# Two blocks of a transformer on one core: the sums of squares of the norms as two rounded terms, and the input norm's statistic inside the tile behind the head

## The reference, cut to what matters

```
def rms_norm(x, g):
    return x * rsqrt(mean(x * x, axis=-1) + NORM_EPS) * g

for layer in range(2):                       # first block
    h = rms_norm(x, mix_pre_g[layer])
    m = hybrid_swa_rwkv(h, ...) if layer == 0 else nsa_layer(h, ...)
    x = x + rms_norm(m, mix_post_g[layer])
    h = rms_norm(x, ffn_pre_g[layer])
    x = x + rms_norm(conv_ffn(h, ...), ffn_post_g[layer])
# second block
h = h + 0.5 * rms_norm(swiglu(rms_norm(h, g1), ...), g1_post)
u = rms_norm(h, mix_norm_pre)
... attention branch and recurrent branch of u @ w_in, merged ...
h = h + rms_norm(merged @ w_out, mix_norm_post)
h = h + 0.5 * rms_norm(swiglu(rms_norm(h, g2), ...), g2_post)
```

## Time and profile before

| | |
|---|---|
| median of three executions | 2860.36 us |
| the profiled execution's own time | 2854.86 us |
| its span | 2853.1 us |
| TensorE (PE) busy | 97% of the span |
| VectorE busy | 51% |
| ScalarE busy | 37% |
| chain that ended last | PE 92%, DVE 4%, ACT 3%, issue 1%, DMA 0% |

### The profile page before, as it was taken

How to read it: one execution, slowest core, us unless ns; L and a number is a source line. 1 busy time by engine, 2 the same in 40 slices (tenths; PEclk the granted TensorE clock), 3 DMA queues, 4 the chain that set the end, 5 groups by cost and what they waited for, 6 DMA issues and landing times.

```text
span 2853.1 us, 38460 instructions
## 1 busy us (share of the span) xinstructions
PE 2780.3 (97%) x16326; PEld 2251.5 (79%) x16326; DVE 1450.4 (51%) x2394; ACT 1061.3 (37%) x1618; POOL 14.6 (1%) x30
## 2 busy tenths in 40 slices
PE   8988999999999999999999999999999999999997
PEld 6787788888887788888887888877788788888886
DVE  5844576543525756655345443284634444654433
ACT  5534453332325654433233222244333422432221
POOL 0000000000000000000000000001000000000000
PEclk9999999999999999999999999999999999999999
DMA  4200122222421002222223222236222122222221
GB/s 149 89 8 3 45 89 96 96 89 96 155 100 36 1 1 96 96 96 89 96 74 111 89 96 96 89 115 123 78 78 85 67 96 96 89 90 95 96 91 65
DMA packets 68861, 238.84 MB, mean 84 GB/s; under 512 B 7976, under 2 KB 10536, under 8 KB 68180
## 3 DMA queue, kind: packets, MB, share of 16 engines
q1 hardware_dynamic: 62064, 220.41, 22.6%
q10 hardware_dynamic: 6628, 15.98, 2.5%
HBM read 228.23 MB, written 6.03 MB: 82 GB/s over the span
## 4 chain that ended last, share of the span: by engine, by line
PE 92%; DVE 4%; ACT 3%; issue 1%; DMA 0%; ACTq 0%; SPq 0%; DVEq 0%
PE psum L153 23%; PE psum L155 23%; PE psum L154 23%; PE psum L1307 3%; PE psum L1274 2%; PE psum L199 2%; PE psum L1294 2%; PE psum L200 2%; PE psum L830 2%; PE psum L207 1%; PE psum L1790 1%; PE psum L176 1%; PE psum L175 1%; PE psum L174 1%; PE psum L1968 1%
## 5 line engine op out<-in xcount | busy, mean ns | idle before, releaser
L153 PE MATMUL psum<-x_hi,w_hi 128*128 128x512 f32 x2120 | 856.1, 404 | 0.2 <-DVE w_lo L128 0.2
L155 PE MATMUL psum<-x_hi,w_lo 128*128 128x512 f32 x2120 | 840.5, 396 | 0.0
L154 PE MATMUL psum<-x_lo,w_hi 128*128 128x512 f32 x2120 | 840.0, 396 | 0.0
L128 DVE TENSOR_TENSOR w_lo<-raw,w_hi 128x1024 fp32r<-128x1024 f32 x409 | 499.5, 1224 | 358.2 <-ACT w_hi L121 358.1
L121 ACT ACTIVATE w_hi<-raw 128x1024 fp32r<-128x1024 f32 x409 | 427.8, 1049 | 343.8 <-DMA raw<-w_down 84.6
L153 PEld LDWEIGHTS psum<-x_hi,w_hi 128*128 128x128 f32 x2120 | 399.5, 188 | 103.2 <-issue 7.2
L154 PEld LDWEIGHTS psum<-x_lo,w_hi 128*128 128x128 f32 x2120 | 399.7, 189 | 98.9 <-issue 5.0
L155 PEld LDWEIGHTS psum<-x_hi,w_lo 128*128 128x128 f32 x2120 | 399.4, 188 | 97.1
L153 PE MATMUL psum<-h_hi,w_hi 128*128 128x512 f32 x616 | 244.3, 397 | 0.0
L155 PE MATMUL psum<-h_hi,w_lo 128*128 128x512 f32 x616 | 244.3, 397 | 0.0
L154 PE MATMUL psum<-h_lo,w_hi 128*128 128x512 f32 x616 | 244.3, 397 | 0.0
(11 more groups left out here) (408 smaller groups left out, 3296.7 us busy)
## 6 DMA issues: line engine op xcount, KB each, us to landing
raw<-w_up SPq DMA_DIRECT2D x88, 512.0 KB, 3.3
raw<-w_down SPq DMA_DIRECT2D x44, 512.0 KB, 3.2
raw<-w_f1up SPq DMA_DIRECT2D x44, 512.0 KB, 3.3
raw<-w_f2up SPq DMA_DIRECT2D x44, 512.0 KB, 3.2
raw<-w_qkv SPq DMA_DIRECT2D x36, 512.0 KB, 3.3
raw<-w_blend SPq DMA_DIRECT2D x28, 512.0 KB, 3.2
raw<-w_f1down SPq DMA_DIRECT2D x22, 512.0 KB, 3.2
raw<-w_f2down SPq DMA_DIRECT2D x22, 512.0 KB, 3.2
```

The source lines that it names most:

```text
L128: dve.tensor_tensor(self.w_lo[u % SLOTS][:], self.raw[u % SLOTS][:], self.w_hi[u % SLOTS][:].bitcast(F32), ALU.subtract).then_inc(self.lo_ ...
L153: pe.matmul(bank[:], hi, x_hi[:, kk], start=kk == 0, stop=False)
L154: pe.matmul(bank[:], hi, x_lo[:, kk], start=False, stop=False)
L155: mm = pe.matmul(bank[:], lo, x_hi[:, kk], start=False, stop=kk == kt - 1)
```

## The change

The sums of squares no longer go through a float32 matmul. ACT rounds `acc` to `acc_hi`, DVE makes `acc_lo` = `acc` - `acc_hi`, and two fp32r matmuls with a rounded copy `mean_r` of the constant are summed in PSUM (`pe_mean`). `acc_lo` lies where `acc` lies and `acc_hi` where `ln` lies. The matmuls on the squares of the last tile (L459, L463) stay float32. In the input statistic, the matmul leaves its place ahead of the head's last four matmuls and goes to the middle of tile 4, the first tile behind the head, ahead of its block 4 (`kk == KD // 2`). For the very first norm (`hybrid_input`) it stays where it was, between tiles 2 and 3.

```diff
-        if not norm.first:
-            self.pe_stat(pe, norm)
         low(last)
 
     def pe_stat(self, pe, norm):
-        pe.wait_ge(self.x_summed, (norm.event + 1) * (KD - 1))
-        pe.matmul(self.stat_bank[:], self.mean[:], self.acc[:], start=True, stop=True).then_inc(self.x_stat, 1)
+        pe.wait_ge(norm.sum_low, norm.event + 1)
+        self.pe_mean(pe, ALL, True).then_inc(self.x_stat, 1)
+
+    def pe_mean(self, pe, c, stop):
+
+        pe.matmul(self.stat_bank[:, c], self.mean_r[:], self.acc_hi[:, c], start=True, stop=False)
+        return pe.matmul(self.stat_bank[:, c], self.mean_r[:], self.acc_lo[:, c], start=False, stop=stop)
+
+    def pe_behind_head(self, pe, g, t, norm):
+
+        self.pe_tile(pe, g, t, (lambda pe, kk: self.pe_stat(pe, norm) if kk == KD // 2 else None) if t == HEADS_OUT else None)
 
     def pe_normed(self, pe, g, norm):
 
         self.pe_head(pe, g, norm)
         for t in range(HEADS_OUT, g.tiles):
-            self.pe_tile(pe, g, t)
+            self.pe_behind_head(pe, g, t, norm)
...
     def end(self, act):
         k = self.k
+        act.wait_ge(k.x_summed, (self.event + 1) * (KD - 1))
+        act.activation(k.acc_hi[:], k.acc[:], ACT.Copy).then_inc(self.sum_high, 1)
         k.act_prepare(act, self.next_unit + SLOTS)
...
+    def low_sum(self, dve):
+        k = self.k
+        dve.wait_ge(self.sum_high, self.event + 1)
+        dve.tensor_tensor(k.acc_lo[:], k.acc[:], k.acc_hi[:].bitcast(F32), ALU.subtract).then_inc(self.sum_low, 1)
...
@@ -385,6 +401,7 @@
         self.low(dve, n - 1)
         self.add_square(dve, KD - 2)
         self.add_square(dve, KD - 1)
+        self.low_sum(dve)
         self.k.dve_prepare(dve, self.next_unit + SLOTS)
...
-        act.wait_ge(summed, s0 + t - 2)
+        act.wait_ge(summed, s0 + KD - 2)
+        act.activation(k.acc_hi[:], k.acc[:], ACT.Copy).then_inc(sum_high, 1)
         act.wait_ge(half_done, e + 1)
         act.activation(k.sq[t % 2][:, TOKENS[0]], banks[0][:, TOKENS[0]], ACT.Square).then_inc(squared, 1)
...
                     if kk == kt - 1 and half == 0:
-                        pe.wait_ge(summed, s0 + KD - 2)
-                        pe.matmul(k.stat_bank[:, TOKENS[0]], k.mean[:], k.acc[:, TOKENS[0]], start=True, stop=False)
+                        pe.wait_ge(sum_low, e + 1)
+                        k.pe_mean(pe, TOKENS[0], False)
...
                         pe.wait_ge(root, r0 + 1)
-                        pe.matmul(k.stat_bank[:, TOKENS[1]], k.mean[:], k.acc[:, TOKENS[1]], start=True, stop=False)
+                        k.pe_mean(pe, TOKENS[1], False)
...
         k.dve_ahead(dve, g, t)
+        dve.wait_ge(sum_high, e + 1)
+        dve.tensor_tensor(k.acc_lo[:], k.acc[:], k.acc_hi[:].bitcast(F32), ALU.subtract).then_inc(sum_low, 1)
         dve.wait_ge(squared, n0 + KD)
...
@@ -1600,7 +1621,7 @@
-            k.pe_tile(pe, g, i)
+            k.pe_behind_head(pe, g, i, norm)
...
+            k.acc_lo, k.acc_hi = sb("acc_lo", [P, T], F32R, s), sb("acc_hi", [P, T], F32R, s)
         k.acc, k.ln, k.r, k.rn = (sb(n, [P, T]) for n in ("acc", "ln", "r", "rn"))
...
             act.wait_ge(set_up, 4)
+            act.activation(k.mean_r[:], k.mean[:], ACT.Copy).then_inc(mean_rounded, 1)
...
             pe.wait_ge(set_up, 4)
+            pe.wait_ge(mean_rounded, 1)
```

More of the change, by code:

```diff
@@ L262, in __init__ @@
         self.term, self.squared, self.root = sem("x_term"), sem("x_squared"), sem("x_root")
+        self.sum_high, self.sum_low = sem("x_sum_high"), sem("x_sum_low")
         self.next_unit = k.units
@@ L418, in residual @@
     squared, summed, stat, root, half_done = (sem(f"post_{n}") for n in ("squared", "summed", "stat", "root", "half_done"))
+    sum_high, sum_low = sem("post_sum_high"), sem("post_sum_low")
     e = k.span("post_events", 1)
@@ L2232, in build @@
         k.ht = [sb(f"ht{j}", [P, T]) for j in range(2)]
+        with ExitStack() as s:
+            k.acc_lo, k.acc_hi = sb("acc_lo", [P, T], F32R, s), sb("acc_hi", [P, T], F32R, s)
         k.acc, k.ln, k.r, k.rn = (sb(n, [P, T]) for n in ("acc", "ln", "r", "rn"))
@@ L2235, in build @@
         k.eps = sb("eps", [P, 1])
+        k.mean_r = sb("mean_r", [P, P], F32R)
         psum = ctx.enter_context(nc.psum_tensor("psum", [P, 8, T], F32))
@@ L2246, in build @@
         loaded, loaded_const, set_up, stored = sem("loaded"), sem("loaded_const"), sem("set_up"), sem("stored")
+        mean_rounded = sem("mean_rounded")
         ffn, L0 = Memory(), Memory()
```

## The result

Six executions of the changed kernel had a median of 2870.19 us (2867.2 to 2871.94), six of the kernel before 2859.07 us (2855.44 to 2861.9). The ratio is 1.0037, with a 95% interval of 1.0027 to 1.0048: +10.6 us, between +7.7 and +13.7. The prediction was +8.5 us and 2868.9.

A forecast was written before the change was run, and what follows sets the result against it. TensorE was taken as the bound, holding 92% of the chain. Terms: +5.7 (waits) - 0.6 - 0.4 (post norms) + 2.0 (`up0`, `up1`) + 3.35 (`xr`) - 4 * 0.39 = +8.5 us, on 2860.36: 2868.9; range 2864 to 2873.

The forecast's parts named there:

- Cheaper matmuls: At input statistics and post norms: two fp32r matmuls save 0.39 us per 512 columns, 0.20 per 256; at most 5.5.
- The wait at three post norms: At 358, 1098 and 2458 us TensorE waits for ACT's rounding and DVE's rest: 2.1 us, 1.9 net each, 5.7 together.
- The drain behind the table load: Rival, 4%: the table load also drains, 1.4 us more at three post norms, +12.7 in all, or 2873.
- The later statistic: At six input statistics Ln, Exp, `rn` and everything behind them come 3.35 us later.
- `up0` and `up1`: TensorE waits 1.4 us for the weight unit of tile 6; less 0.39, +1.0 each, 2.0 for both.
- `f1up`, `f2up` and `nsa_in`: Weight units still in time despite the later statistic, so no wait: -0.39 us each.
- `xr`: DVE is the chain there, so the later statistic counts whole, +3.35 us; wait of 3.9 at tile 6.
- the second wait in `xr`: At the gate matmul L1790 TensorE waits 3.4 us for DVE.
- rival 4: Rival, 3%: a 2 us wait lowers TensorE's clock, costing some microseconds at each of five places; 2875 or more.

The follow-up runs named there:

- block 0: The changed kernel with the input statistic's matmuls ahead of block 0 of tile 4 in place of block 4: 2864.45 us, ratio 1.0014 against before.
- block 6: The changed kernel with the input statistic's matmuls ahead of block 6 of tile 4 in place of block 4: 2877.18 us, ratio 1.0060 against before.
- the issues behind the tile: Against two-term kernel with statistic in place, rounding ahead of table load, later mean: `xr`'s five loads issued behind ScalarE's first tile; 2854.60 us, 0.9975 of before.

## Why the prediction was right

- **Cheaper matmuls.** 0.39 for 512 columns: 0.38 to 0.40 in every stretch of the kernel with the input statistics alone. 0.20 for 256 columns ahead of a down product's post norm: -0.22 at all three in the kernel with the post norms alone. L480's part is swallowed at the post norms with a head: the wait for `x_hi` is 0.52 and not 0.33.
- **The wait at three post norms.** 2.1 us for the weight load, by ACT's table load, rounding and rest: measured 2.04, and 1.89 net at the first and third, 1.91 at the second (1.9 predicted). None behind the down products (the shortest distance there from load to mean is 3.48 us, at 1474, and not 3.54, which was still enough). Taking the rounding ahead of the load and the mean later (both costs taken out) removes this loss, so its cause is shown. What the sum left out is the clock behind it, below.
- **The drain behind the table load.** The rounding began at 360.09, 0.01 behind the load's end at 360.08, and the load itself began 0.02 behind the end of the instruction ahead of it. The Trainium skill has a drain of about 1380 ns with each such load ("ScalarE: Activation LUTs", What ACT_TABLE_LOAD costs). The trace doesn't agree; by that rule 1.4 us would have come on top, and the measurement decides.
- **The later statistic.** 3.35 predicted, 3.35 or 3.36 in all six.
- **`up0` and `up1`.** 1.4 predicted, waits of 1.33 and 1.32. `f1up`, `f2up` and `nsa_in`: none, as predicted. Their stretch is 0.16 shorter than my sum (-4.10 + 3.35 = -0.75 against -0.59); the float32 form in the same place shows it too (-3.89 + 3.74 = -0.15), block 0 doesn't. Most of it lies in the last tile of the down product: 96 of its half matmuls in a row (1838.15 to 1849.54 us in the kernel before) take 0.12 us less in the changed kernel and in the one with the move alone. Why they do stays open.
- **`xr`.** +3.35 predicted. From the post norm's second Ln (1863.81) to the gate matmul (1932.93) it is 69.12 us, before from 1856.67 to 1922.49 65.82: +3.30. The first wait is 3.88 (3.9 predicted).
- **Wrong: the second wait in `xr`**, 0.91 in place of 3.4. The step that failed is rival 4, which I gave 3%: "behind the wait of 3.37 the granted clock stays 1.00, so the waits here should not". Behind the wait of 3.88 it was 0.50, and twelve distances of 0.43 rather than 0.234 make TensorE some 2.4 us later at the gate matmul. DVE is the bound there, so it came out of the second wait (0.91 + 2.4 = 3.3) and cost nothing. I had named DVE as the bound of `xr`, but not that it would hide a fall of the clock: that the total came out right in spite of this step is luck.
- **Left out: the clock behind the new wait of the post norms.** Rival 4 was put aside with the wait of 3.37 in `xr`, but the same trace had waits of 2.32 us (at 299) and 2.48 us (at 2016) with the lower clock behind them. The rows of PE and of the clock in the kernel before:

```profile
299.34 1.99 PE L1114 MATMUL psum<-rw_sg,z 128*128 128x512 f32 x2 [2.32 <-DVE ht L1157]
...
299.30:303.00 3.70, 3.66 (x12) 2.51 (x14) 1.32 (x6) 2.10 (x6) 0.00 (x0) 0.54 0.00 0
2015.70:2020.00 4.30, 4.26 (x11) 2.41 (x11) 2.17 (x5) 1.28 (x1) 0.00 (x0) 0.60 0.00 0
```

Four profiled kernels have the new wait at three post norms. The clock fell there at none in the changed kernel, at one with post norms alone, at all three with block 0 and at two with block 6: 6 of 12. In the six profiles without that wait, the stretch from the square of tile 6 to Ln is 4.71 to 4.76 us at all 18. A fall cost 0.9 to 1.6 us more at its post norm.

The sum of +8.5 lies inside the measured +7.7 to +13.7. The 2.1 between it and the middle isn't shown in a trace, since the one profile of the changed kernel had no such fall. An estimate from the counts above gives about the right size: half of three post norms, at 1.27 us on average, is 1.9 us. The granted clocks point the same way: 0.990 to 0.993 in the six executions of the changed kernel, 0.992 to 0.996 in the 54 of the kernel before.

## What to carry to other kernels

A cheaper form of an operation must be charged with the hand-overs between engines that it adds: here two rounded terms saved 5.5 us on TensorE at the most, and at three places added two hops behind a table load, at 1.9 us each. Before a statistic is moved "into the shadow" of a matmul, follow what starts with its result, down to the first thing that TensorE wants from that list; here it was a weight unit behind six instructions of DVE, taken in turn with ACT's, and the slack was 2.0 us for a delay of 3.35. A new wait can also cost more than its length, when the clock falls behind it. And cut two traces at marks that repeat to 0.02 us, so that a change of 0.3% can be read from one profile even where whole executions scatter as much.

## What the runs showed of the hardware

TensorE's clock after a wait isn't settled by the wait alone. Behind the same wait of the post norms (1.84 us in TensorE's row, 2.04 in that of its weight load) the granted clock stayed 1.00 at six places and was 0.62 or 0.63 over 4.5 us at six others. Behind waits of 1.33 and 0.86 us it stayed 1.00 in the stretches shown. Behind 2.70, 2.72 and 3.88 it was 0.54, 0.59 and 0.50, so near the lower level of 1.2 GHz. Behind about the same wait at the gate matmul of `xr`, the kernel before had 1.00 once (3.37) and 0.70 the second time (3.43):

```profile
1928.71 3.53 PE L1790 MATMUL psum<-lru_xc,lru_wx 128*128 128x512 f32 x4 [3.43 <-DVE rel_rv L1830]
...
1928.70:1934.00 5.30, 5.29 (x9) 2.47 (x10) 3.54 (x4) 1.06 (x1) 0.44 (x1) 0.70 0.51 57
```

There four matmul records took 3.53 us in place of 1.98. That the clock of a stretch differs from one execution to the next is also what the stretch from 280 to 340 us shows, with 0.97 and 0.89 for the same kernel. Over whole executions, 0.992 to 0.996 goes with 2864.94 to 2855.65 us, as the table by granted clock shows.

ScalarE took up the next instruction 0.01 us behind the end of a table load of 1.28 us (360.08 to 360.09). The time that its five DMA issues took in `xr` differed: the first tile came 4.02 us behind Ln in the changed kernel, 4.08 before, 4.63 with block 0, and 2.12 with the issues behind the tile.
